# One group of attention scores, the input stage, an output tile and the recurrence's first group moved, and two recurrence levels copied by ACT

## The reference

```python
def stick_breaking_mixer(q, k, v):             # block 1, 4 heads
    z = einsum('bqhd,bkhd->bhqk', q_blk, k) * scale
    log_1m = where(strict, log_sigmoid(-z), 0.0)
    rem = lax.cumsum(log_1m, axis=3, reverse=True) - log_1m
    a = where(strict, exp(log_sigmoid(z) + rem), 0.0)
    return einsum('bhqk,bkhd->bqhd', a, v)

# block 1: y = rms_norm of each of 4 groups; x = x + y @ w_out
# block 1, start: h = rms_norm(x, norm1_w); cols = h @ w_in
# block 2, one direction of the recurrence, per head:
#   S_t = diag(f_t) S_(t-1) + k_t v_t^T,  o_t = S_t^T q_t,  with k_t = 1 - f_t
```

## Time and profile before

| | us |
|---|---|
| median of 3 runs | 1802.92 (1802.78 to 1804.18) |
| profiled execution | 1803.52 |
| its span | 1801.4 |
| mean granted PE clock | 0.988 |

### The profile page before, as it was taken

How to read it: one execution, slowest core, us unless ns; L and a number is a source line. 1 busy time by engine, 2 the same in 40 slices (tenths; PEclk the granted TensorE clock), 3 DMA queues, 4 the chain that set the end, 5 groups by cost and what they waited for, 6 DMA issues and landing times.

```text
span 1801.4 us, 20984 instructions
## 1 busy us (share of the span) xinstructions
PE 1737.8 (96%) x8107; PEld 1376.0 (76%) x8107; DVE 969.2 (54%) x1724; ACT 692.2 (38%) x1243; POOL 203.3 (11%) x167
## 2 busy tenths in 40 slices
PE   7999999999999999999999899999999999999998
PEld 4557778566888888887788787775887888888887
DVE  4465476343563333346655788875444555556334
ACT  3233344552433233234464545552424422223234
POOL 3233100002100000012000233320200200000000
PEclk9999999899999999999999999999999999999999
DMA  6243201213433323233122011113330223332221
GB/s 186 80 132 95 94 24 48 76 59 99 126 94 94 102 94 108 95 94 98 55 70 71 12 59 59 48 59 99 123 106 1 94 94 97 106 101 94 94 94 47
DMA packets 122371, 152.23 MB, mean 85 GB/s; under 512 B 8827, under 2 KB 110609, under 8 KB 121762
## 3 DMA queue, kind: packets, MB, share of 16 engines
q1 hardware_dynamic: 119986, 140.19, 24.5%
q0 software_dynamic: 2288, 10.71, 1.7%
HBM read 144.90 MB, written 6.00 MB: 84 GB/s over the span
## 4 chain that ended last, share of the span: by engine, by line
PE 89%; DVE 5%; ACT 2%; issue 2%; DMA 1%; POOL 0%; DVEq 0%; ACTq 0%; POOLq 0%
PE bank L1953 50%; PE bank L1987 16%; PE bank L1261 2%; PE bank L1654 2%; PE bank L2198 2%; PE bank L2309 2%; PE bank L1212 1%; PE bank L2282 1%; PE bank L2195 1%; PE bank L774 1%; PE bank L1124 1%; PE bank L1129 1%; PE bank L1351 1%; PE bank L1687 1%; PE bank L2084 1%
## 5 line engine op out<-in xcount | busy, mean ns | idle before, releaser
L1953 PE MATMUL bank<-act_high,w_high 128*128 128x512 f32 x1360 | 553.0, 407 | 13.2 <-issue 4.6
L1953 PE MATMUL bank<-act_high,w_low 128*128 128x512 f32 x1360 | 533.1, 392 | 0.0
L1953 PE MATMUL bank<-act_low,w_high 128*128 128x512 f32 x1360 | 532.3, 391 | 0.0
L643 ACT ACTIVATE w_high<-ring 128x1024 fp32r<-128x1024 f32 x222 | 234.4, 1057 | 680.9 <-PE bank L1953 466.9
L667 DVE TENSOR_TENSOR w_low<-ring,w_high 128x1024 fp32r<-128x1024 f32 x202 | 254.7, 1262 | 221.9 <-ACT w_high L643 221.9
L1953 PEld LDWEIGHTS bank<-act_high,w_high 128*128 128x128 f32 x1360 | 257.6, 189 | 75.0 <-issue 16.8
L1953 PEld LDWEIGHTS bank<-act_high,w_low 128*128 128x128 f32 x1360 | 256.7, 189 | 55.2
L1953 PEld LDWEIGHTS bank<-act_low,w_high 128*128 128x128 f32 x1360 | 257.8, 190 | 51.8 <-issue 3.6
L1987 PE MATMUL bank<-act_high,w_high 128*128 128x512 f32 x416 | 162.2, 390 | 2.4 <-DVE arena L3192 1.2
L1987 PE MATMUL bank<-act_high,w_low 128*128 128x512 f32 x416 | 162.0, 389 | 0.0
L1987 PE MATMUL bank<-act_low,w_high 128*128 128x512 f32 x416 | 162.0, 389 | 0.0
(11 more groups left out here) (361 smaller groups left out, 2187.8 us busy)
## 6 DMA issues: line engine op xcount, KB each, us to landing
ring<-in_ffn_w SPq DMA_DIRECT2D x32, 1024.0 KB, 5.3
ring<-in_w_in SPq DMA_DIRECT2D x28, 1024.0 KB, 5.4
ring<-in_w_up SPq DMA_DIRECT2D x22, 1024.0 KB, 5.1
ring<-in_w_down SPq DMA_DIRECT2D x11, 1024.0 KB, 5.0
ring<-in_w_mem_kv SPq DMA_DIRECT2D x8, 1024.0 KB, 5.4
ring<-in_cmp_w SPq DMA_DIRECT2D x4, 1024.0 KB, 7.9
ring<-in_w_out SPq DMA_DIRECT2D x4, 1024.0 KB, 5.5
ring<-in_w_mix_out SPq DMA_DIRECT2D x4, 1024.0 KB, 5.3
```

What stands on the lines that cost most here:

```text
L643: nc.scalar.activation(part(w_high, name), raw_part(name), ACT.Copy).then_inc(w_rounded, 1)
L1953: last = nc.tensor.matmul(b[0:rows, :], w[:, k, 0:rows], a, start=k == 0 and n == 0, stop=k == KT - 1 and n == 2)
```

## The change

It has five parts.

1. cq0 and cq1 get banks of their own (4 and 5). SP asks for cq0's weights ahead of x's second half. ACT rounds them after two squares; POOL splits cq0 and cq1 ahead of the load of `hot`; PE works parts of cq0 and cq1 between the turning of x and the square sums.
2. Three memsets of DVE go from ahead of the rotary step to behind the convolution gates.
3. Memory keys are spread over units 13 to 54. The scores of stick head 0 are issued by PE at units 58 to 61 into banks 2 and 4, their logs by ACT at units 60 to 63.
4. wo1's first six parts are done ahead of parts 6 and 7 of wo0.
5. The windowed attention's last key tile goes to `strips`, its values to `cmp_bias` and `in_rb`, so that the buffers of the recurrence are free. Floor, log and scan of group 0 go into units 87, 89 and 90, its first three POOL subtractions are no longer held back by the last values, and its first two exps and products go into units 92 to 95. Levels 6 and 7 of each group are copied by ACT (`block_keep`): the pairs of a level are square blocks, two of 32 x 32 at level 6 and one of 64 x 64 at level 7 in each chunk, and are copied as such, without a mask.

```diff
@@ -433,9 +433,9 @@
-        plan("cq0", "dve")
+        plan("cq0", "dve", in_bank=4)
         plan_bias(0, "strip")
-        plan("cq1", "dve")
+        plan("cq1", "dve", in_bank=5)
         plan_bias(0, "fwd")
...
@@ -1342,16 +1342,18 @@
-        def stick_scores(eng, h, between=None):
-            for kt in range(TT):
-                n = 4 * h + kt
-                if n >= 2:
-                    eng.wait_ge(sb_zs, n - 1)
-                r = head_rows(h)
-                nc.tensor.matmul(bank[n % 2][:, 0:ST_W[kt]], ar(SKT + h // 2)[r, kt * P:(kt + 1) * P],
-                                 ar(SQT + h // 2)[r, kt * P:S], start=True, stop=True).then_inc(sb_z, 1)
-                if between:
-                    between(eng, kt)
+        def stick_bank(n):
+            return bank[(2, 4)[n % 2] if n < TT else n % 2]
+        def stick_score(eng, h, kt):
+            n = 4 * h + kt
+            if n >= 2:
+                eng.wait_ge(sb_zs, n - 1)
+            r = head_rows(h)
+            nc.tensor.matmul(stick_bank(n)[:, 0:ST_W[kt]], ar(SKT + h // 2)[r, kt * P:(kt + 1) * P],
+                             ar(SQT + h // 2)[r, kt * P:S], start=True, stop=True).then_inc(sb_z, 1)
@@ -1377,19 +1379,18 @@
-        def stick_logs(eng, h):
-            for kt in range(TT):
-                n = 4 * h + kt
-                eng.wait_ge(sb_z, n + 1)
-                if h >= 2:
-                    eng.wait_ge(sb_o, h - 1)
-                z, s = stick(h, kt, 0), stick(h, kt, 1)
-                nc.scalar.activation(z, bank[n % 2][:, 0:ST_W[kt]], ACT.Copy).then_inc(sb_zs, 1)
-                eng.wait_ge(sb_zs, n + 1)
-                link(eng, "act", nc.scalar.activation(s, z, ACT.Abs))
-                link(eng, "act", nc.scalar.activation(s, s, ACT.Exp, scale=-1.0))
-                nc.scalar.activation(s, s, ACT.Ln, bias=one_col).then_inc(sb_l, 1)
+        def stick_log(eng, h, kt):
+            n = 4 * h + kt
+            eng.wait_ge(sb_z, n + 1)
+            if h >= 2:
+                eng.wait_ge(sb_o, h - 1)
+            z, s = stick(h, kt, 0), stick(h, kt, 1)
+            nc.scalar.activation(z, stick_bank(n)[:, 0:ST_W[kt]], ACT.Copy).then_inc(sb_zs, 1)
+            eng.wait_ge(sb_zs, n + 1)
+            link(eng, "act", nc.scalar.activation(s, z, ACT.Abs))
+            link(eng, "act", nc.scalar.activation(s, s, ACT.Exp, scale=-1.0))
+            nc.scalar.activation(s, s, ACT.Ln, bias=one_col).then_inc(sb_l, 1)
@@ -1421,9 +1422,10 @@
         K_RAW = 27
-        KA = (24, 25, 26, 28)
-        va = ar(29, 3)[:, 0:5 * 64 * TT].rearrange("p (t a c) -> p t a c", a=5, c=64)
-        va_flat = ar(29, 3)[:, 0:5 * 64 * TT]
+        KA = (ar(24), ar(25), ar(26), tile(strips, 3))
+        va_of = [cmp_bias[:, 2 * S + 320 * t:2 * S + 320 * (t + 1)] for t in range(3)] + [in_rb[:, 0:320]]
+        va_parts = [(slice(0, 3), cmp_bias[:, 2 * S:2 * S + 960].rearrange("p (t a c) -> p t a c", a=5, c=64)),
+                    (slice(3, 4), in_rb[:, 0:320].rearrange("p (t a c) -> p t a c", a=5, c=64))]
         MEMQ = 0
...
@@ -1639,6 +1642,28 @@
+        DVE_LEVELS = 6
+        def level_kept(eng, at):
+            g, i = divmod(at, 8)
+            if i < DVE_LEVELS:
+                eng.wait_ge(level_out, DVE_LEVELS * g + i + 1)
+            else:
+                eng.wait_ge(level_act, 2 * g + i - DVE_LEVELS + 1)
+        def block_keep(eng, g, i):
+            eng.wait_ge(level_mm, 8 * g + i + 1)
+            eng.wait_ge(level_out, DVE_LEVELS * (g + 1))
+            w, d = 1 << (i - 1), g % 2
+            src = bank[(8 * g + i) % 2][:, :].rearrange("p (c t) -> p c t", t=P)
+            dst = G_SCORE[d].rearrange("p (c t) -> p c t", t=P)
+            for at in range(0, P, 2 * w):
+                keys, qs = slice(at + w * d, at + w * d + w), slice(at + w * (1 - d), at + w * (1 - d) + w)
+                ins = nc.scalar.activation(dst[keys, :, qs], src[keys, :, qs], ACT.Copy)
+            ins.then_inc(level_act, 1)
         def level_scores(eng, g, i):
@@ -1647,7 +1672,7 @@
             if at >= 2:
-                eng.wait_ge(level_out, at - 1)
+                level_kept(eng, at - 2)
             for c in range(TT):
@@ -1665,14 +1690,15 @@
             else:
-                eng.wait_ge(level_out, at)
+                eng.wait_ge(level_out, DVE_LEVELS * g + i)
                 mask = const(f"lv{'fb'[g % 2]}{i - 1}").bitcast(U32).unsqueeze(1).to_broadcast([P, TT, P])
...
-            eng.wait_ge(level_out, 16 * h + 16)
+            eng.wait_ge(level_out, DVE_LEVELS * (2 * h + 2))
+            eng.wait_ge(level_act, 4 * h + 4)
             eng.wait_ge(states_out, 2 * h + 2)
@@ -1729,7 +1755,8 @@
         STICK_TURN_AT = (5, 9)
-        MEM_KEY_AT = [13 + 8 * i // 5 for i in range(32)]
+        MEM_KEY_AT = [13 + 43 * i // 32 for i in range(32)]
+        STICK_AT = 58
@@ -1806,14 +1833,10 @@
         def _(eng):
-            for half in range(2):
+            def fetch_input(half):
                 ds = slice(half * S, (half + 1) * S)
                 eng.dma_start(x_tok[:, :, ds], A["x"][0].rearrange("(t p) d -> p t d", p=P)[:, :, ds]).then_inc(x_in[half], 16)
-                if half == 0:
-                    eng.wait_ge(cols_zero, 1)
-                    dst, src = gain_load
-                    eng.dma_start(dst, src).then_inc(gain_in, 16)
-            eng.dma_start(rel_sb[0:32, :], A["rel_bias"]).then_inc(rel_in, 16)
@@ -1821,7 +1844,14 @@
-            for i in range(len(loads)):
+            fetch_input(0)
+            eng.wait_ge(cols_zero, 1)
+            dst, src = gain_load
+            eng.dma_start(dst, src).then_inc(gain_in, 16)
+            fetch(0)
+            fetch_input(1)
+            eng.dma_start(rel_sb[0:32, :], A["rel_bias"]).then_inc(rel_in, 16)
+            for i in range(1, len(loads)):
                 if i == SLOTS:
@@ -1839,6 +1869,7 @@
             link(eng, "pool", nc.gpsimd.memset(cmp_bias[64:P, :], 0.0))
+            split_weights(eng, "cq1")
             eng.wait_ge(x_in[1], 16)
@@ -1887,18 +1918,21 @@
             in_parts(eng, "h31")
-            link(eng, "pool", nc.gpsimd.memset(va[:, :, 0:5:2, :], 0.0))
+            filled(eng, "dn7")
+            for _, dst in va_parts:
+                link(eng, "pool", nc.gpsimd.memset(dst[:, :, 0:5:2, :], 0.0))
             for i in range(4):
-                link(eng, "pool", nc.gpsimd.memset(ar(KA[i])[64:P] if i % 2 == 0 else ar(KA[i])[0:64], 0.0))
+                link(eng, "pool", nc.gpsimd.memset(KA[i][64:P] if i % 2 == 0 else KA[i][0:64], 0.0))
             nc.gpsimd.memset(small[:, 62:63], 0.0).then_inc(gqa_zero, 1)
...
             eng.dma_start(rb[:, :], A["consts"][:, c0:c0 + 2 * S]).then_inc(carry_in, 16)
-            eng.wait_ge(pv_mm, N_GQA)
             for g in range(8):
                 for n in range(LEVELS):
+                    if (g, n) == (0, N_X - 1):
+                        eng.wait_ge(pv_mm, N_GQA)
                     level_sub(eng, g, n)
-                    if n == 1:
+                    if n == (1 if g else N_X - 1):
                         rec_end_diff(eng, g)
...
@@ -2085,11 +2113,20 @@
-            features("cq0", big="in1")
+            features("cq0", big="in1", ks=(0, 1))
+            square_sum(eng, 2)
+            square_sum(eng, 3)
+            for k in range(4, 8):
+                turn_input(k)
+            features("cq0", big="in1", ks=(2, 3))
+            square_sum(eng, 4)
+            features("cq1", 108, ks=range(4))
+            square_sum(eng, 5)
+            features("cq0", big="in1", ks=range(4, 8))
             square_sum(eng, 6)
...
             bias_tables(0, "strip")
-            features("cq1", 108)
+            features("cq1", 108, ks=range(4, 8))
             bias_tables(0, "fwd")
...
@@ -2209,13 +2248,19 @@
                     mem_pair(eng, MEM_KEY_AT.index(u))
+                if STICK_AT <= u < STICK_AT + TT:
+                    if u < STICK_AT + 2:
+                        taken(eng, f"memk{6 + u - STICK_AT}")
+                    stick_score(eng, 0, u - STICK_AT)
             attend_pe(eng, 0, N_B1, ahead_by=2, between=mem_key_pair)
-            eng.wait_ge(head_out, 4)
-            stick_scores(eng, 0)
             for h in range(4):
                 if h + 1 < 4:
-                    stick_scores(eng, h + 1, lambda eng, kt: mem_pair(eng, 32 + 8 * h + kt))
+                    for kt in range(TT):
+                        stick_score(eng, h + 1, kt)
+                        mem_pair(eng, 32 + 8 * h + kt)
+                if h == 0:
+                    eng.wait_ge(head_out, 4)
                 if h in (1, 2):
@@ -2227,8 +2272,10 @@
             norm_sums(eng, "y3")
-            features("wo0", parts="y", ks=(6, 7))
-            for m in range(1, 8):
+            features("wo1", parts="y", ks=range(6))
+            for m in range(2):
+                features(f"wo{m}", parts="y", ks=(6, 7))
+            for m in range(2, 8):
                 features(f"wo{m}")
@@ -2368,18 +2415,22 @@
```

(57 more changed lines are left out.)

22 lines of the change are left out of this document (10 added, 12 removed).

## The result

The changed kernel takes **1781.8 us** (median of four runs, 1781.0 to 1782.8) against 1802.9: a ratio of 0.9876, 95% interval 0.986 to 0.989. Predicted were 1791.3 and a range of 1782.5 to 1798.5. It is 21 us faster instead of 12, just outside the range.

What follows compares the result with a forecast made beforehand. PE bounds the kernel, busy 1737.8 of 1801.4 us, so only its idle time and low clock can be won. 3.6 + 0.2 + 4.5 + 5.8 + 0 - 2.5 = 11.6 off 1802.9 gives 1791.3, range 1782.5 to 1798.5.

Steps and rivals of the forecast that it cites:

- Part 1: Input stage: earlier cq0 weights let PE begin cq0 at 15.1; gain 3.6 us, between 1.5 and 5.
- Part 2: DVE's memsets ahead of the rope, moved later: PE's wait there stays; gain 0.2 us, between 0 and 1.5.
- Part 3: Last output norm: wo1 matmuls fill PE's wait, 1.1 appears ahead of wo2; gain 4.5 us, between 3 and 5.
- Part 4: Recurrence's start: first group begun early inside the last attention units; gain 5.8 us, between 3 and 7.
- Part 5: Recurrence: two levels kept by ACT instead of DVE; no change in time, between -4 and +4 us.
- Part 6: Stick scores inside attention: 13.3 us lost for 10.8 before if the clock falls; a loss of 2.5, 0 to 5.
- PE's work in it: Last attention units with head 0's logs: PE works 6.9 us there, leaving 5.3 idle.
- the clock falls, since the gaps are alike: Stick scores: half busy stretch brings clock 0.50 again, losing 6.7 + 0.5 us; chance 0.43.
- Rival B: Stick scores: clock stays up despite three gaps of about 2 us, +4.7 there, 1784.1 us in all; chance 0.34.

Runs made afterwards that it cites:

- Experiment 10: Changed kernel with ACT's q1 norm factor ahead of the weights' rounding: 1774.3 us; with recurrence keys turned behind level 4's projection: 1779.6; with both: 1769.6.
- experiment 3: Changed kernel with two further ACT Abs passes over head 0's logs of key tiles 0, 1 and 2: 1793.4, 1785.7, 1793.7 and 1788.9 us.
- Experiment 9: Changed kernel measured once more, unchanged: 1779.7, 1779.5, 1781.4, 1787.5 and 1782.8 us.
- experiment 4: Kernel before with three 512-column matmuls, read by nothing, laid into PE's two waits at the stick scores: 1797.0 us.
- experiment 1: Changed kernel with the stick move alone taken back (head 0's scores and logs behind attention, memory pairs at old places): 1792.3 us.
- experiment 5: Kernel before with the input stage's move alone (m_q ahead of x's second half, cq0 rounded after two squares): 1798.6 us.
- experiment 6: Kernel before with wo1's first six rows alone laid into the wait of the last output norm: 1801.6 us.

## Why the prediction was wrong, and where it was right

**Part 1, input stage: right.** 3.6 forecast, 3.5 found without the stretch at 67.6, 5.0 with it. cq0 was rounded at 10.6 instead of 11.6, but PE began at 14.96 for the forecast 15.1, because the last thing to come was no longer the weights: it was the low half of x (L965 on DVE), which hangs on the gain columns that PE itself turns at 12.76. A rival for the end of the wait (the gain chain) was missing from the working; the result hid it. The last sum of squares ended at 32.0 (31.9). The 1.5 of the stretch at 67.6, which all ten traces with the move lack, were not forecast.

**Part 2, DVE's fills: right.** The wait at the turned memory tile is 4.5 (4.3 before). Experiment 10 shows whose it is: ACT's factor behind a rounding that waits for its load, as the prediction's chain had it, and not DVE's fills.

**Part 3, wo1: right.** 4.5 forecast, 4.1 found twice, with the 1.2 (1.1 forecast) ahead of wo2.

**Part 4, first group: right.** 5.8 forecast, 5.8 by the two traces, 5.5 by holding it back. PE waits 0.9 for DVE's normalised probabilities ahead of a turn (L1201; the forecast had it at the copy behind the turn) and 0.7 for ACT's last heads (1.5 forecast together).

**Part 5, ACT's block copies: right at the value, and the range was far too wide.** ACT +6.6 (7), DVE -12.4 (12), time nothing.

**Part 6, the stick scores: wrong, by 11 us,** 8.7 of gain for a loss of 2.5. The length of the stretch was right: 12.3 us from the first log to the end of attention (12.2). **The step that failed is "PE's work in it": 6.9 us forecast, 10.65 found.** The prediction took over the work of the old stretch, which begins with a unit's values. But ACT is at its first log at 313.90, when PE still has a score and a turn to do ahead of those values (0.9), and three of the four stick scores fell inside (2.0) where 0.65 was booked. Another 0.5 was misread in the rows: the three memory pairs were taken off at 1.03 us each, the length of their rows, but the next matmul starts 0.86 after a pair does (320.83 and 321.69), so they gave back 2.6 and not 3.1. The last 1.0 is that matmuls in short runs each take a little longer: four value matmuls of a unit that stand between two waits take 0.71 (322.08), and took 0.45 to the next start where work followed at once (322.02 in the kernel before). So PE stood still for 1.6 us in gaps of 0.3 to 0.8 and not 5.3 in gaps of 2, and for 0.6 ahead of it (0.8 forecast): 3.9 of the 11. The other 7.2 are the clock. The step "the clock falls, since the gaps are alike" rested on that size. For gaps of the size it was right in part: experiment 3 made two of that kind and got the long fall in the profiled run and, by the mean clocks, in two runs of four. In the changed kernel the longest gap is 0.8, and the clock stayed at 1.00. Rival B named the result (the clock stays up), but for another reason than the one found: it trusted broken gaps of 2 us to be harmless, and priced the idle time at the same 6.1.

The Trainium skill (TensorE: Matmul & The Clock Gate, section What's actually happening) has the clock go down after an idle stretch and up after a busy one, and says that the stretch it looks at does not start with the kernel, so that the turning point differs from run to run. Experiment 9 agrees with the last: the same two gaps of 0.9 us, a clock of 0.87 in one execution and 1.00 in the other. That a busy stretch brings the clock up is not what experiment 3 shows, where 15.0 of 15.0 busy us stayed at 0.50.

**The sum.** 3.6 + 0.2 + 4.5 + 5.8 + 0 - 2.5 = 11.6 was forecast; 3.5 + 0 + 4.1 + 5.8 + 0 + 8.7 = 22.1 is the trace, and with 1.5 for the low stretch that the input stage's move took away and 3.3 off for the two in the recurrence that come and go, 20.3. The range's lower end was rival B's time less 1.6; with 8.7 instead of 4.7 for part 6, B would have stood at 1780.1 and the end at 1778.5. The range had no term at all for the scatter of the low stretches, and nine runs of the changed kernel span 1779.5 to 1787.5.

## What to carry to other kernels

When work is moved into a stretch, list what each engine still has queued at the moment the stretch begins, instead of taking over the busy time of the old one: an idle time is a difference of two large numbers. Gaps of PE of one to two microseconds can cost their length about twice over again when the stretch behind them then runs at the low clock (3.8 us of gaps, 7.0 of clock in the kernel before; three matmuls that fill the two longer ones made it 7.1 us faster), so fill the gaps ahead of a long stretch first. Put nothing that others wait for behind an instruction that waits for a load.

## What the runs showed of the hardware

- The low clock can outlast the gaps ahead of it by far: 23.9 us, 15.0 of them with PE busy throughout, and the same scores and memory pairs ran 16.0 of 16.0 us at 1.00 when the clock had not fallen before them (experiment 4). In experiments 1, 3 and 5 and in the kernel before it came back 1.5 to 2.2 us after the first suffix sum (L1364 of the kernel before at 346.2, the clock at 347.7), but in experiment 6 0.4 us ahead of it, so the suffix sums are not what brings it back. What does is open.
- The same kernel, with the same gaps, gets other low stretches in other executions, mostly of 3.4 us (1.7 us of loss each). Two kernels that differ by under 3 us can't be told apart by the span of one profile of each; the waits and the leads at fixed instructions tell them apart.
- Which decides for a fall, the longest gap or their sum, stays open: it fell within a gap of 2.3 (experiment 3) and at the end of one of 1.8 with one of 0.7 ahead of it (before), and stayed up with 0.3, 0.4, 0.4 and 0.8 at the same place; in the recurrence two of 0.9 did either. The gap alone does not decide: one of 1.0 us, at 62 to 69, was followed by a fall in the four traces without the input stage's move and in none of the ten with it.
